# DeltaNet of a hybrid encoder layer: decay columns made once for all heads, work of three queues moved, and identity transposes put on TensorE inside the inverse

## The reference, cut to what matters

```python
g = jnp.cumsum(g, axis=-1)                      # log decay inside a chunk
decay = jnp.exp(jnp.where(incl, g[..., :, None] - g[..., None, :], -jnp.inf))
k_beta = k * beta[..., None]
a_mat = jnp.einsum("bhnid,bhnjd->bhnij", k_beta, k) * jnp.where(strict, decay, 0.0)
sol = lax.linalg.triangular_solve(eye + a_mat, rhs, left_side=True, lower=True, unit_diagonal=True)
qk = jnp.einsum("bhnid,bhnjd->bhnij", q, k) * decay
q_dec = q * jnp.exp(g)[..., None]
k_dec = k * jnp.exp(g_last - g)[..., None]
# then over chunks: v_new = u - w s; o = q_dec s + qk v_new; s = s exp(g_last) + k_dec^T v_new
```

## Time and profile before

| | |
|---|---|
| median of three runs | 3056.8 us |
| the profiled execution's own time | 3061.3 us |
| its span, first to last instruction | 3059.6 us |
| TensorE busy / VectorE / ScalarE / GpSimd | 94% / 42% / 35% / 39% |
| mean granted TensorE clock, as a share of full | 0.968 |
| DeltaNet in the profile | about 1244 to 1647 us |

### The profile page before, as it was taken

One profiled execution on the slowest core, in us unless ns is written; L12 is line 12 of the kernel. 1 busy time (PEld: TensorE's weight loads), 2 busy tenths in 40 slices (PEclk: granted clock), 3 DMA queues, 4 the chain that ended last, 5 costly groups with the idle time before them and its releaser, 6 DMA issues. The chain is left out here.

```text
span 3059.6 us, 38554 instructions
## 1 busy us (share of the span) xinstructions
PE 2888.3 (94%) x15219; PEld 2356.4 (77%) x15219; DVE 1299.4 (42%) x1953; ACT 1072.4 (35%) x1829; POOL 1206.5 (39%) x805
## 2 busy tenths in 40 slices
PE   6999999999999969578778999999999999999998
PEld 5878787877888846477667887878888888888887
DVE  5233233321479949666564353322233232232323
ACT  4241313243044539455544122332333333333232
POOL 2222122121123320423421433466666666766663
PEclk9999999999999979878798999999999999999999
DMA  4434233343545357210103546332322333332331
GB/s 114 165 132 140 80 102 102 100 132 94 184 148 176 120 189 249 80 44 31 73 31 126 179 141 208 105 100 93 102 91 91 103 96 124 97 97 91 114 110 58
DMA packets 239571, 352.78 MB, mean 115 GB/s; under 512 B 32928, under 2 KB 186272, under 8 KB 239392
## 3 DMA queue, kind: packets, MB, share of 16 engines
q1 hardware_dynamic: 239392, 350.32, 35.2%
HBM read 263.71 MB, written 96.36 MB: 118 GB/s over the span
## 5 line engine op out<-in xcount | busy, mean ns | idle before, releaser
L102 PE MATMUL pj_acc<-u_hi,pj_w_hi 128*128 128x512 f32 x1464 | 576.6, 394 | 10.6 <-DVE u_lo L823 10.6
L2763 DVE TENSOR_TENSOR x_tm<-m_ps,x_tm 128x512 f32<-128x512 f32 x384 | 265.0, 691 | 745.8 <-PE m_ps L104 745.8
L104 PE MATMUL pj_acc<-u_hi,pj_w_lo 128*128 128x512 f32 x1464 | 571.9, 391 | 0.0
L103 PE MATMUL pj_acc<-u_lo,pj_w_hi 128*128 128x512 f32 x1464 | 571.7, 391 | 0.0
L551 POOL TENSOR_TENSOR pj_w_lo<-pj_w_raw,pj_w_hi 128x1024 fp32r<-128x1024 f32 x61 | 159.2, 2610 | 722.0 <-ACT pj_w_hi L600 722.0
L2645 POOL TENSOR_TENSOR m_lo<-gate,held 128x1024 fp32r<-128x1024 f32 x96 | 237.8, 2500 | 270.0 <-ACT held L2562 270.0
L102 PEld LDWEIGHTS pj_acc<-u_hi,pj_w_hi 128*128 128x128 f32 x1464 | 275.9, 188 | 85.7 <-issue 18.2
L104 PEld LDWEIGHTS pj_acc<-u_hi,pj_w_lo 128*128 128x128 f32 x1464 | 276.1, 189 | 58.2
L103 PEld LDWEIGHTS pj_acc<-u_lo,pj_w_hi 128*128 128x128 f32 x1464 | 276.2, 189 | 56.2
L102 PE MATMUL m_ps<-held 128*128 128x512 f32 x768 | 299.7, 390 | 2.4 <-DVEq L2744 2.4
L102 PE MATMUL m_ps<-held,m_h_hi 128*128 128x512 f32 x768 | 299.5, 390 | 0.0
(11 more groups left out here) (308 smaller groups left out, 4939.8 us busy)
## 6 DMA issues: line engine op xcount, KB each, us to landing
gate<-in_w_mlp_dram SPq DMA_DIRECT2D x48, 1024.0 KB, 5.4
gate<-in_w_mlp_dram SPq DMA_DIRECT2D x96, 512.0 KB, 3.7
proj<-pj_stage SPq DMA_DIRECT2D x61, 768.0 KB, 3.4
pj_w_raw<-in_w_in_dram SPq DMA_DIRECT2D x61, 512.0 KB, 5.2
gate<-proj SPq DMA_DIRECT2D x24, 768.0 KB, 4.4
mo_w_raw<-in_w_out_dram SPq DMA_DIRECT2D x48, 256.0 KB, 2.9
rpb_bias<-pj_shut SPq DMA_DIRECT2D x48, 192.0 KB, 3.1
rpb_bias<-rpb_near SPq DMA_DIRECT2D x24, 384.0 KB
```

What stands on the lines that cost most here:

```text
L102: pe.matmul(out, w_hi, x_hi, start=first, stop=False)
L103: pe.matmul(out, w_hi, x_lo, start=False, stop=False)
L104: return pe.matmul(out, w_lo, x_hi, start=False, stop=last)
L2763: dve.tensor_tensor(xt, ps2[:, q % 4], xt, ALU.add).then_inc(added, 1)
```

## The change

1. **Columns.** `decay_columns` goes. The ends of all heads' decays come from one pair of TensorE products (a one-hot matrix, copied from `ident` into `work`, by `cols`) at the start of DeltaNet, followed by five VectorE operations (`columns`), one exponential over all heads and one product (`rates`). Beta moves into the exponent: `gbeta` = ln(max(beta, 1e-30)) + g is made in attention, so `scores` is one operation of 128 x 512 a unit in place of four of 128 x 128.
2. **Queues.** ScalarE's exponentials of the decay rows move from inverse steps 0 and 2 to recurrence steps 5 and 6 of the head before; one decay group moves out of the inverse; the cut comes before the output copies on ScalarE and after the state updates on VectorE; GpSimd's product into gq is cut in three; ScalarE takes 4 of the copies of `place`; lengths come 4 columns at a time; the steps of the output normalisation and of TOKEN_AT and TURN_AT are set anew, the gate at step 15 where it was at 12.
3. **Idle transposes.** TensorE issues 40 transposes of `ident` (WARM) into bank 7 ahead of step 0 of each inverse, and 4 into ps[:, k % 2] ahead of each S(k), between the wait for the bank and the wait for the operands: 72 + 40 a head.

```diff
@@ attention, VectorE and ScalarE
+            dve.tensor_scalar(gbeta[:], cols[:, :, 2:4], 1e-30, None, ALU.max).then_inc(d_rates, 1)
+            dve.tensor_scalar(gneg[:], cols[:, :, 0:2], -1.0, None, ALU.mult).then_inc(d_cols, 1)
                 if u == DCOL_AT:
-                    dve.wait_ge(dg_in, 32)
-                    dc = Chain(dve, d_chain, 0, 8)
-                    decay_columns(dve, dc, cols[:, 0], col2[:, 0], ncol2[:, 0], cx2[:, 0], gq[:, 0])
+                    dve.wait_ge(d_rates, 2)
+                    dve.tensor_tensor(gbeta[:], cols[:, :, 0:2], gbeta[:], ALU.add).then_inc(d_cols, 1)
+            act.wait_ge(d_rates, 1)
+            act.activation(rates, rates, ACT.Ln).then_inc(d_rates, 1)
@@ constants
-SQUARES_AT, ROOT_AT, EG_AT, CEXP_AT = 1, 5, (0, 2), 10
-LENGTHS_AT, MEAN_AT, DIAG_AT, SPREAD_AT, NORM_AT, GATE_AT = 2, 3, 5, (7, 9, 11), (8, 10, 12), 12
-TURN_AT = (0, 3, 6, 9, 11, 13)
-TOKEN_AT = ((1, 2), (4, 5), (7, 8), (10, 11), (12, 13), (14, 15))
-INCL_AT = {8: 4, 11: 5, 13: 0, 15: 1}
+SUM_AT, SQUARES_AT, LENGTHS_AT, MEAN_AT, ROOT_AT, DIAG_AT = 0, 2, (3, 4, 5), 6, 8, 8
+SPREAD_AT, NORM_AT, GATE_AT = (10, 12, 14), (11, 13, 15), 15
+TURN_AT = (0, 2, 5, 8, 11, 13)
+TOKEN_AT = ((0, 1), (2, 3), (5, 6), (9, 10), (11, 12), (13, 14))
+INCL_AT = {9: 4, 12: 5, 15: 0}
-INCL_END = {1: 3, 3: 2}
+INCL_END = {1: 1, 3: 3, 4: 2}
-QK_IN = {0: (4, 5), 1: (0, 1), 4: (3, 2)}
+QK_IN = {0: (4, 5), 2: (0, 1), 5: (3, 2)}
+WARM = 40
+EG_IN = (5, 6)
@@ ScalarE: place (row_decays(i + 1, d) now stands in recurrence steps 5 and 6)
-                act.wait_ge(S["spread"], 2 * i + 2)
+                act.wait_ge(S["spread"], 2 * i + 1)
+                for q in Q32:
+                    act.copy(by_direction(un, q, 0)[:, 0:NTB:2, :, q], compact(c1, q, 0)[:, 0:NTB:2]).then_inc(S["un0_d0"], 1)
+                act.wait_ge(S["spread"], 2 * i + 2)
@@ TensorE
+                for j in range(WARM):
+                    pe.transpose(ps[:, 7, j % 4], ident[:], ident[:])
                 for step in range(NS + T_LAG):
                     if step < NS:
                         k, n = step, ORDER[step % NG6]
+                        if k >= 2:
+                            pe.wait_ge(S["s_ev"], i * NS + k - 1)
+                        for j in range(4):
+                            pe.transpose(ps[:, k % 2, j], ident[:], ident[:])
+            pe.wait_ge(S["ends"], 2)
+            for d in range(2):
+                last = pe.matmul(ps[:, 3, d, 0:HEADS * NT], work[:, d * P:(d + 1) * P], cols[:, :, d], start=True, stop=True)
+            last.then_inc(S["ends"], 1)
             for x in range(NTB):
                 gram(0, x)
@@ VectorE
-                for j in range(4):
-                    last = dve.scalar_tensor_tensor(am[:, n, j], ps[:, 4 + 2 * (GRAMS.index(tg) % 2), j],
-                                                    ncol2[:, i % 2, 2 + d, 4 * tg + j:4 * tg + j + 1], decays[:, j], ALU.mult, ALU.mult)
-                last.then_inc(S["am_done"], 1)
+                dve.scalar_tensor_tensor(am[:, n], ps[:, 4 + 2 * (GRAMS.index(tg) % 2)], -1.0, decays, ALU.mult,
+                                         ALU.mult).then_inc(S["am_done"], 1)
-                    if k == COLUMNS_AT and more:
-                        columns(i + 1, nxt)
+                    if more and step == CUT_IN:
+                        cut_blocks(i + 1)
             dve.wait_ge(S["prm_in"], 16)
+            for d, row in ((0, P - 1), (1, 0)):
+                dve.tensor_copy(work[:, d * P:(d + 1) * P], ident[:, row:row + 1].to_broadcast([P, P])).then_inc(S["ends"], 1)
```

More of the change, by code:

```diff
@@ L1861, in out_gate, with columns, rates @@
                 dve.scalar_tensor_tensor(oc[0], oc[0], 0.5, zt, ALU.mult, ALU.mult).then_inc(S["out_done"], 1)
-            def columns(i, c):
-                dve.wait_ge(S["g_in"], i * 32 + 32)
-                decay_columns(dve, c, cols[:, i], col2[:, i % 2], ncol2[:, i % 2], cx2[:, i % 2], gq[:, i % 2])
-                dve.sem_inc(S["cols_in"], 1)
+            def columns():
+                c = Chain(dve, S["columns"], 0, 5)
+                c.add(dve.tensor_copy(cx[:, :, 0:2], cols[:, :, 0:2]))
+                dve.wait_ge(S["ends"], 3)
+                for d in range(2):
+                    ends = ps[:, 3, d, 0:HEADS * NT].rearrange("p (h t) -> p h t", h=HEADS)
+                    c.add(dve.tensor_tensor(cx[:, :, 2 + d], ends, cols[:, :, d], ALU.subtract))
+                    c.add(dve.tensor_copy(cx[:, :, 4 + d], ends))
+                c.end()
+            def rates():
+                dve.wait_ge(S["cexp"], 1)
+                dve.scalar_tensor_tensor(cx[:, :, 0:2], cols[:, :, 2:4], -1.0, cx[:, :, 0:2], ALU.mult, ALU.mult).then_inc(S["columns"], 1)
+                dve.wait_ge(S["columns"], 6)
             def scores(i, n):
-                tg, d = UN[n]
+                tg = UN[n][0]
                 decays = am[:, n] if i else dd0[:, 2 * n]
@@ L1948, in prepare, with main @@
                     narrow(i)
[L1949 to L1953 removed]
+            def main(i, more):
                 for k in range(NS):
@@ L1997, in main @@
                         if step:
-                            dve.scalar_tensor_tensor(st[:, j], st[:, j], cx2[:, i % 2, EGL[d], t:t + 1], ps[:, j, 2], ALU.mult, ALU.add).then_inc(S["st_ev"], 1)
+                            dve.scalar_tensor_tensor(st[:, j], st[:, j], cx[:, i, EGL[d], t:t + 1], ps[:, j, 2], ALU.mult, ALU.add).then_inc(S["st_ev"], 1)
                         else:
                             dve.tensor_copy(st[:, j], ps[:, j, 2]).then_inc(S["st_ev"], 1)
+                    if more and step == CUT_IN:
+                        cut_blocks(i + 1)
                 if more:
-                    place(i + 1, False)
-                c.end()
+                    place(i + 1)
             dve.wait_ge(S["prm_in"], 16)
-            chains = [Chain(dve, S["chain"], i, K_DN) for i in range(HEADS)]
+            for d, row in ((0, P - 1), (1, 0)):
+                dve.tensor_copy(work[:, d * P:(d + 1) * P], ident[:, row:row + 1].to_broadcast([P, P])).then_inc(S["ends"], 1)
             dve.memset(ps[:, 0:2], 0.0).then_inc(S["blank"], 1)
-            dve.sem_inc(S["chain"], 8)
-            chains[0].n = 8
-            dve.sem_inc(S["cols_in"], 1)
-            for part in range(STEPS):
-                prepare(0, part, chains[0])
-            place(0, False)
+            for step in range(STEPS):
+                prepare(0, step)
+                if step == 0:
+                    columns()
+                if step == CUT_IN:
+                    cut_blocks(0)
+                if step == WIDE_IN:
+                    rates()
+            place(0)
             for i in range(HEADS - 1):
-                main(i, True, chains[i], chains[i + 1])
-            main(HEADS - 1, False, chains[HEADS - 1], None)
+                main(i, True)
+            main(HEADS - 1, False)
             dve.wait_ge(S["gated"], HEADS)
```

138 lines of the change are left out of this document (58 added, 80 removed).

## The result

The changed kernel takes 3083.0 us (3082.3 to 3084.6, four runs) beside 3056.0 us for the one before: ratio 1.0086, 95% interval 1.0074 to 1.0098. It is slower by 0.9%, and the prediction (3036.6, range 3015 to 3057) was wrong in size and in sign. The profiled execution took 3084.6 us.

The account below looks back on a forecast made before the run. TensorE was taken as the bound, with its clock, waits and pauses to win in the inverses. Terms -6 + 2 - 6.2 - 5 - 5 = -20.2 took the median from 3056.8 to 3036.6 us, range 3015 to 3057.

Parts of the forecast that it names:

- part 4: Four recurrences: -5 us from starts at full clock and -5 us from less VectorE work in the early steps.
- part 3: Four DeltaNet inverses: clock gains outweigh added transposes and waits, heads at -2.5, -3.6, -3.5 and +3.4, sum -6.2 us.
- GpSimd's three pieces and the loads of y keep their slack of a whole inverse: Recurrences: the divided GpSimd product and the loads of y have ample time; no cost was entered.
- The new split of `place` would be ready earlier than that and is worth nothing more: Pause before inverses: warm transposes start heads 1 to 3 1.3 us later; sharing the placing copies gains nothing.
- they cost nothing, and up to 1 us a head if that cover is gone: Recurrence steps 5 and 6: moved decay rows are ScalarE work beside a chain leaving it nearly 2 us.
- the kept waits: Rival: VectorE and ScalarE keep TensorE waiting, transposes come on top, clock drops before recurrences; 3053 us, chance 0.20.
- the slow rival of 3091: Rival: idle transposes do not hold TensorE's clock, so they are added cost in the inverses; +34, 3091 us, chance 0.10.
- Does a transpose hold the clock?: Inverses: assumed idle transposes count as work and the clock stays full from the first of them on.
- Part 1: Attention: removing `decay_columns` ends a 5.43 us TensorE idle and the half clock after it; -6 us, bounds -4 and -8.
- Part 2: Start of DeltaNet: later gram products and column operations, less shorter `scores`; net +2 us, bounds 0 and +4.
- VectorE -5: Recurrences: shorter `scores`, later cut and no `widen` wait save about 1.7 us for each of three heads; bounds -1 and -7.
- Clock -5: Recurrence starts: 17.4 us at half clock would run at full, 6.6 us less, taken as -5; bounds 0 and -6.6.

Follow-up runs that it names:

- GpSimd held: Changed kernel, but GpSimd begins a head's decayed queries only when VectorE has placed the whole inverse start: 3045.3 us, ratio 0.9962.
- experiment 4: Kernel before the change plus only the idle transposes, 40 ahead of each inverse and 4 a step: 3078.3 us, ratio 1.0070.
- 11: Changed kernel with GpSimd's queries held until placing is done, 3 idle identity products a step replacing the 4 transposes, warm 40 kept: 3056.2 us, ratio 0.9994.
- experiment 3: Changed kernel with GpSimd's queries held until placing is done and no idle transposes: 3031.8 us, ratio 0.9922.
- experiment 13: Changed kernel, all transposes kept, only GpSimd's masks held until VectorE's placing is done, queries free: 3068.5 us, ratio 1.0033.

## Why the prediction was wrong, point by point

A ledger from TensorE's timelines, from its first S product of head 0 to the merge (the merge's first product is at 1651.0 us before). The idle 4.2 us between the last product of the recurrences and the merge are alike in all three and left out. "Inverses" runs from the first S product to the first product behind the last U, "recurrences" from there to their last product. The predicted column is the working on record, sorted into these parts, the pause taken out of the inverses.

| us against before | predicted | changed kernel | the same, GpSimd held |
|---|---|---|---|
| start of head 0 (parts 1 and 2) | -4 | -5.2 | -7.0 |
| four inverses (190.7 before) | -10.1 | **+24.1** | -16.1 |
| four recurrences (158.3) | -10 | +3.5 | +4.0 |
| three pauses (15.0) | +3.9 | +1.0 | +1.0 |
| sum | -20.2 | +23.4 | -18.1 |

**The step that failed** is in part 4 and part 3: "GpSimd's three pieces and the loads of y keep their slack of a whole inverse", and "The new split of `place` would be ready earlier than that and is worth nothing more". The first counted only who waits for GpSimd's result. It did not ask what runs on VectorE while GpSimd works, and the move of the decay rows, costed as ScalarE work only ("they cost nothing, and up to 1 us a head if that cover is gone"), takes away the 4.3 us in which GpSimd was idle beside the placing. That is worth 37.7 us by the hold (40.0 without transposes), and both the undoing of the move (25.4 us in three heads) and the half hold (14.5) fit. The row was to be had: GpSimd's idle time beside 16 quick copies. Of the 46.4 us between forecast and measurement the hold gives back 37.7; the other 8.7 stay, and part 4 below is the largest miss among them. None of the rivals on record was this one. The sign of the kept waits did show (TensorE waits 11.9 us in each of inverses 1 and 2), but that rival stopped at 3053 and had other causes; the slow rival of 3091 rested on the clock.

The Trainium skill (SBUF — State Buffer, Who interferes with whom) says that VectorE and GpSimd share a pair of ports which one instruction holds to its end while the other blocks, and that VectorE's copies can be of that sort. By that rule each copy beside GpSimd would take about one GpSimd instruction; the traces agree, 1.17 to 1.21 us against 1.25. The lock itself no trace here shows.

**Does a transpose hold the clock?** Right, by experiment 4 (0.50 became 1.00 in nearly the same stretch, and 1.00 through a pause filled with transposes alone) and 11. But "the clock stays full" was too strong: it fell to 0.50 behind the wait of 5.0 us above, and the inverses came to 0.81 to 0.88 in the changed kernel and 0.95 to 0.99 with GpSimd held.

**Part 1, attention, -6.** Right. VectorE's last copy of attention starts at 1243.96 before and 1236.86 after, -7.1. The one operation left there takes 1.02 us (0.95 was reckoned), and the stretch of the earlier trace rows runs at full clock. The row of VectorE and the window, in the changed kernel:

```profile
1130.64 1.02 DVE L1226 TENSOR_TENSOR dn_gbeta<-cols,dn_gbeta 128x96 f32<-128x96 f32 x1
```

```profile
1139.70:1145.70 6.00, 6.00 (x54) 3.41 (x48) 5.31 (x24) 5.84 (x23) 0.00 (x0) 1.00 0.45 118
```

**Part 2, +2.** Right within its bounds: the start of head 0 keeps -5.2 (-7.0 held) of those 7.1. The step inside was off: the gram products begin 2.1 us sooner, so 5.0 of attention's 7.1 are used up ahead of them, where 2.8 were reckoned. The two one-hot copies took 2.49 us, while GpSimd cleared buffers; that this is the same collision in small was not tested. The timelines of VectorE and TensorE answer to the earlier trace rows:

```profile
1242.38 2.49 DVE L2013 COPY dn_work<-ident 128x128 f32<-128x128 f32 x2 [5.23 <-DMA dn_nw<-in_dn_norm_dram]
```

```profile
1245.82 8.44 PE L1728 MATMUL dn_ps<-dn_yn 128*128 128x128 f32 x48
```

**Part 3, the inverses.** With the collision gone the heads take 35.9, 47.2, 47.1 and 44.4 us, where 40.0, 45.5, 46.6 and 46.5 were forecast (pause taken out, and cut as in the earlier trace rows, 2.0 us shorter in all than here): 174.6 against 178.6 in sum. The waits of heads 1 and 2 are 5.7 us, where 3.5 was taken. One of these waits is the gate at step 15, which the prediction did see: TensorE waits 2.50 us at the end of inverse 1, while VectorE runs these, in the changed kernel:

```profile
1424.27 1.76 DVE L1863 SCALAR_TENSOR_TENSOR oz<-oz 128x1536 f32<-128x1536 f32 x1
1426.06 0.88 DVE L1968 COPY dn_un<-dn_ps 64x256 f32<-64x256 f32 x2
```

So the length was right, but not what earned it. The forecast set 35 us of clock against 42.4 of transposes. In fact the other parts of the change, with the collision gone, raised the clock of heads 0 to 2 without any idle transposes (experiment 3), and all idle transposes together are a net cost of 10 to 13.5 us. Fewer waits look like the cause, and are in part: the hold alone cut TensorE's waits in inverses 1 and 2 from 13.9 and 14.1 us to 6.2 and 9.8 while the clock rose from 0.73 and 0.63 to 0.81 and 0.89. But the sum of the waits doesn't settle it, since in head 2 it is 9.7 us before the change as well, at a clock of 0.76, and in head 3 the hold cut it from 10.9 to 7.6 while the clock fell from 0.74 to 0.68. Which waits matter stays open. The warm 40 were reckoned at 1.3 us a head against the old pause; against the pause that the split placing allows they cost 2.8 to 3.1, the second quoted sentence again.

**Part 4, the recurrences, -10.** Wrong, +3.5 to +4.0 in either kernel. "VectorE -5" is nothing: from its second step on the recurrence of head 1 takes 33.3 us before and after. VectorE had 2.6 us less of `scores`, and its state updates waited 3.7 us longer for TensorE instead (7.4 against 3.7). It was not the bound, so this term should have been nothing. "Clock -5" came only in head 0, which has no gate ahead of it (first products to second step 8.6 us before, 6.4 after); in heads 1 and 2 these grew by 1.1 to 1.4 us, in head 1 with a clock of 0.71 behind the gate's stall (0.81 before). In head 3 they grew by 2.0, at 0.54 in either kernel. There it is a wait: TensorE stands idle 1.78 us for a copy of ScalarE (`nb`, line 1659), which itself waited 7.29 us until the late gate's output was stored. Before the change no such wait of TensorE stands there. This price of the gate at step 15 was in no sum.

**The sum.** With GpSimd held the profiled execution is 17.7 us below that of before, and the medians 12.0 (0.38%), against 20.2. That these come so near is partly luck: beside the one step above, parts 3 and 4 erred by 6 and 14 us in opposite directions, and the start of head 0 and the pauses gave 6 us more than was forecast.

## What to carry to other kernels

When work is moved earlier, look not only at who waits for it but at what it will now run beside: GpSimd work with slack of a whole stage can still cost TensorE 9 to 12 us a head when it lands on VectorE's short copies. An idle gap of GpSimd beside a quick burst of VectorE can be part of what makes the burst quick. And ahead of idle work for the clock, measure the kernel without it: here the moved queues and the hold raised the clock of the first two inverses from 0.70 to above 0.80, and idle work on top was a loss of 10 us or more, although it does hold the clock.

## What the hardware showed that was not expected

- Forty transposes in a row take 4.56 us at full clock, 0.114 each, where four between other products take 0.147.
- VectorE's placing copies take 1.0 to 1.2 us beside GpSimd's queries and masks and 0.22 to 0.31 without, four to five times as long, though the two engines touch different tiles. GpSimd's six pieces took 7.57 us in the collision, 1.26 each.
- Some versions spread more from run to run than others: 3029.3 to 3042.0 over nine executions of the best one, 3025.2 to 3044.4 for that with the early gate, and 3034.3 to 3054.0 with the 40 warm transposes alone, while five of the held version with all its transposes lie within 2.7 us. It is not the transposes alone that decide, since the version of experiment 13 has all of them and spreads over 12.5. The inverse of head 3 at 0.68 or head 2 at 0.76 is the likely place; what decides it stays open. The profiled execution of experiment 3 was its slowest, 7.5 us over its median, so profiles show a smaller gap between 1 and 3 than the medians.
